# A two-block network with routed experts on one core: VectorE sums the even gathered rows, GpSimd scales and adds the odd ones

## What is computed

```python
def one_block(xb):                                   # 128 tokens
    q = (xb @ w_query).reshape(tb, PEER_HEADS, 2, PEER_KEY_DIM // 2)
    s = jnp.einsum('thpd,hpnd->thpn', q, sub_keys)
    ...                                              # per head the best 16 of 128 x 128 experts
    gate = jax.nn.softmax(best_s, axis=-1)
    u = jnp.take(expert_down, eid, axis=0)
    act = jax.nn.gelu(jnp.einsum('thkd,td->thk', u, xb), approximate=False)
    v = jnp.take(expert_up, eid, axis=0)
    return jnp.einsum('thk,thkd->td', gate * act, v)
```

## Time and profile before

| | us |
|---|---|
| median of 3 runs | 3384.24 (3382.91 to 3390.31) |
| profiled execution | 3385.41 |
| its span in the trace | 3383.5 |

### The profile page before, as it was taken

One profiled execution on the slowest core, in us unless ns is written; L12 is line 12 of the kernel. 1 busy time (PEld: TensorE's weight loads), 2 busy tenths in 40 slices (PEclk: granted clock), 3 DMA queues, 4 the chain that ended last, 5 costly groups with the idle time before them and its releaser, 6 DMA issues.

```text
span 3383.5 us, 48188 instructions
## 1 busy us (share of the span) xinstructions
PE 3248.1 (96%) x16264; PEld 1958.5 (58%) x16264; DVE 2223.6 (66%) x4855; ACT 1193.5 (35%) x3181; POOL 833.5 (25%) x686
## 2 busy tenths in 40 slices
PE   9999998999999999989999999999899999999997
PEld 4444567656666666656445544456755666666664
DVE  2064698997888776773133400269899778877777
ACT  1141105895445550011022200110589545555001
POOL 0000244433333333320000000024443333333332
PEclk9999999999999999989999999999999999999998
DMA  4153227999999999982211122122899999999997
GB/s 175 75 224 137 75 87 311 387 414 395 418 416 415 398 400 421 422 357 88 82 50 56 62 75 74 62 108 88 315 384 418 394 396 422 417 401 400 419 422 321
DMA packets 130830, 929.03 MB, mean 275 GB/s; under 512 B 15072, under 2 KB 15968, under 8 KB 19072
## 3 DMA queue, kind: packets, MB, share of 16 engines
q0 software_dynamic: 73728, 536.90, 38.7%
q1 hardware_dynamic: 53280, 379.61, 28.3%
q10 hardware_dynamic: 3680, 10.84, 0.9%
HBM read 925.17 MB, written 2.12 MB: 274 GB/s over the span
## 4 chain that ended last, share of the span: by engine, by line
PE 54%; DMA 14%; DVE 9%; issue 9%; ACT 1%; DVEq 1%; POOL 1%; POOLq 0%; ACTq 0%
PE proj L560 17%; PE proj L854 14%; DMA ring<-in_experts,idx 14%; PE obk L845 8%; PE proj L552 4%; PE proj L778 3%; DVE ring L1740 3%; DVE xn L1757 3%; PE tps L807 2%; PE proj L916 1%; PE tps L980 1%; PE obk L959 1%; PE proj L742 1%; PE proj L949 1%; DVE hT L1776 1%
## 5 line engine op out<-in xcount | busy, mean ns | idle before, releaser
L468 POOL DMA_INDIRECT ring<-in_experts,idx x512 | 679.3, 1327 | 1225.5 <-DVE xn L1757 1117.3
L854 PE MATMUL proj<-wring,hT 128*128 128x512 f32 x2048 | 948.8, 607 | 14.6 <-DVE hT L1799 14.0
L1740 DVE SCALAR_TENSOR_TENSOR ring<-ring,xn 128x1024 f32<-128x1024 f32 x512 | 608.5, 1221 | 174.1 <-DMA ring<-in_experts,idx 170.3
L845 PE MATMUL obk<-hT,wring 128*128 128x256 f32 x3072 | 694.2, 379 | 0.0
L845 PEld LDWEIGHTS obk<-hT,wring 128*128 128x128 f32 x3072 | 583.5, 190 | 159.7 <-issue 86.8
L1757 DVE SCALAR_TENSOR_TENSOR xn<-ring,coef,xn 128x1024 f32<-128x1024 f32 x512 | 628.7, 1280 | 20.9 <-DVE coef L1747 1.0
L854 PEld LDWEIGHTS proj<-wring,hT 128*128 128x128 f32 x2048 | 377.0, 192 | 397.9 <-issue 375.0
L1222 ACT ACTIVATE hot<-iotab,away 128x128 bf16<-128x128 bf16 x1792 | 548.6, 391 | 0.1
L560 PE MATMUL proj<-hT,wring 128*128 128x512 f32 x1120 | 487.3, 592 | 0.0
L489 POOL TENSOR_TENSOR ring<-ring 128x2048 bf16<-128x2048 bf16 x14 | 56.8, 4059 | 1264.3 <-DVE ring L1700 1264.3
L560 PEld LDWEIGHTS proj<-hT,wring 128*128 128x128 f32 x1120 | 211.4, 190 | 257.1 <-issue 256.8
(11 more groups left out here) (290 smaller groups left out, 2319.9 us busy)
## 6 DMA issues: line engine op xcount, KB each, us to landing
wring<-in_slabs SPq DMA_DIRECT2D x355, 1024.0 KB, 8.9
ring<-in_experts,idx POOLq DMA_INDIRECT x512, 10.1
x_res<-in_x SPq DMA_DIRECT2D x4, 512.0 KB, 13.5
ring<-in_keys ACTq DMA_DIRECT2D x2, 1024.0 KB, 6.8
out<-x_res SPq DMA_DIRECT2D x4, 512.0 KB, 2.6
ring<-ada_rows ACTq DMA_DIRECT2D x1, 1536.0 KB, 6.4
hT<-in_xT SPq DMA_DIRECT2D x1, 1024.0 KB, 10.5
ring<-in_norm_pre ACTq DMA_DIRECT2D x2, 512.0 KB, 10.4
```

The costliest lines, as they stand in the source:

```text
L468: pool.indirect_dma_start(rows[:, r, :], None, d[f"experts{layer + 1}"], bass.IndirectOffsetOnAxis(idx[:, k, r:r + 1], 0)).then_inc(row[r] ...
L845: m = pe.matmul(obk[:, j % 2, 0:DT], wring[:, k, at + c * P:at + (c + 1) * P], hT[:, c, GB * P:T], start=(c == 0), stop=(c == DC - 1))
L854: m = pe.matmul(proj[:, 2 * b + c, :], coefs[:, b * P:(b + 1) * P], wring[:, k, at + c * 512:at + (c + 1) * 512], start=False, stop=False, ...
L1740: v.scalar_tensor_tensor(rows[:, r, 0:D], rows[:, r, 0:D], 1.0, xn[:, r % GB, :], ALU.mult, ALU.mult, accum_out=dots[:, r:r + 1]).then_inc ...
```

## The change

GpSimd gets the sums of the odd rows. For each odd row it runs a TENSOR_SCALAR, the `v` half times the coefficient, in place, and a TENSOR_TENSOR that adds the result to `gathered[:, 1, :]`, with waits between them on new counters. VectorE's `row_sums` does only even rows, into `gathered[:, 0, :]`. `slot_free` becomes `even_summed` and `odd_summed`; a gather waits for the counter of its own parity. GpSimd's odd sums for a group of the unit before stand directly ahead of that group's three gathers of the next unit. The rest of the diff moves the initial counts.

```diff
+                def odd_sums(u, r, h):
+                    pool.wait_ge(coef_done, u * 2 + (layer * GROUPS + h + 1))
+                    pool.sem_inc(sum_paced, 1)
+                    pool.tensor_scalar(rows[:, r, D:2 * D], rows[:, r, D:2 * D], coef[:, r:r + 1], None, ALU.mult).then_inc(odd_scaled, 1)
+                    pool.wait_ge(odd_scaled, u * GROUP + (layer * HALF_ROWS + r // 2 + 1))
+                    pool.sem_inc(sum_paced, 1)
+                    pool.wait_ge(odd_summed, u * GROUP + (layer * HALF_ROWS + r // 2 + GROUP))
+                    pool.sem_inc(sum_paced, 1)
+                    pool.tensor_tensor(gathered[:, 1, :], gathered[:, 1, :], rows[:, r, D:2 * D], ALU.add).then_inc(odd_summed, 1)
...
                     for r in range(n):
-                        pool.wait_ge(slot_free, u * RING + (layer * GB * SLOTS + r + 1))
+                        if before is not None and r % GROUP == 0:
+                            for o in range(r, r + GROUP):
+                                if o % 2:
+                                    odd_sums(before, o, r // GROUP)
+                        pool.wait_ge(odd_summed if r % 2 else even_summed, u * GROUP + (layer * HALF_ROWS + r // 2 + 1))
                         pool.sem_inc(paced, 1)
                         pool.indirect_dma_start(
...
-                with pool.Fori(0, UNITS // 2) as it:
+                unit(0, 0, RING, None)
+                with pool.Fori(0, UNITS // 2 - 1) as it:
                     for k in range(2):
-                        unit(it * 2 + k, k, RING)
-                unit(UNITS, 0, TAIL)
+                        unit(it * 2 + (k + 1), (k + 1) % 2, RING, it * 2 + k)
+                unit(UNITS - 1, 1, RING, UNITS - 2)
+                unit(UNITS, 0, TAIL, UNITS - 1)
+                for r in range(1, TAIL, 2):
+                    odd_sums(UNITS, r, 0)
...
                 for r in range(h * GROUP + first, h * GROUP + n):
-                    v.wait_ge(slot_free, u * RING + (layer * GB * SLOTS + r - 1 + RING))
-                    v.scalar_tensor_tensor(gathered[:, r % GB, :], rows[:, r, D:2 * D], coef[:, r:r + 1], gathered[:, r % GB, :],
-                                           ALU.mult, ALU.add).then_inc(slot_free, 1)
+                    if r % 2 == 0:
+                        v.wait_ge(even_summed, u * GROUP + (layer * HALF_ROWS + r // 2 + GROUP))
+                        v.scalar_tensor_tensor(gathered[:, 0, :], rows[:, r, D:2 * D], coef[:, r:r + 1], gathered[:, 0, :],
+                                               ALU.mult, ALU.add).then_inc(even_summed, 1)
```

More of the change, by code:

```diff
@@ L38 @@
 UNITS, TAIL = divmod(GB * SLOTS, RING)
+HALF_ROWS = SLOTS
 GROUPS = 2 * UNITS + 1
@@ L343, in build @@
         z_done, z_act, coef_t_ready = sem("z_done"), sem("z_act"), sem("coef_t_ready")
-        slot_free, acc_done, acc_free = sem("slot_free"), sem("acc_done"), sem("acc_free")
+        acc_done, acc_free = sem("acc_done"), sem("acc_free")
+        even_summed, odd_summed, odd_scaled, sum_paced = sem("even_summed"), sem("odd_summed"), sem("odd_scaled"), sem("sum_paced")
         zeros_set, out_ready, paced = sem("zeros_set"), sem("out_ready"), sem("paced")
@@ L458, in gather, with unit @@
                 pool.sem_inc(paced, 1)
-                def unit(u, k, n):
+                def odd_sums(u, r, h):
[7 more added lines that the diff above has]
+                    pool.tensor_tensor(gathered[:, 1, :], gathered[:, 1, :], rows[:, r, D:2 * D], ALU.add).then_inc(odd_summed, 1)
+                def unit(u, k, n, before):
                     pool.tensor_copy(idx[:, k, 0:n], flat[:, bass.ds(u * RING, n)]).then_inc(idx_ready, 1)
@@ L1454, in _ @@
                 root(rstd[:, tb:tb + 1], ss[:, tb:tb + 1], D, rms_done)
-            act.wait_ge(slot_free, 2 * GB * SLOTS + RING)
+            act.wait_ge(even_summed, 2 * HALF_ROWS + GROUP)
+            act.wait_ge(odd_summed, 2 * HALF_ROWS + GROUP)
             for tb in range(GB):
@@ L1476, in _ @@
             v.memset(epsc2, EPS * EPS)
-            for k, (s, n) in enumerate(((mm_free, 4), (key_done, 4), (key_free, 4), (slot_free, RING), (spread_done, 2),
+            for k, (s, n) in enumerate(((mm_free, 4), (key_done, 4), (key_free, 4), (even_summed, GROUP), (odd_summed, GROUP), (spread_done, 2),
                                         (spread_free, 2), (z_act, 4), (coef_t_ready, 2))):
-                v.memset(zeros[:, 80 * k:80 * (k + 1)], 0.0).then_inc(s, n)
+                v.memset(zeros[:, 72 * k:min(72 * (k + 1), P + 512)], 0.0).then_inc(s, n)
             v.memset(silz[:, :, :], 0.0)
@@ L1861, in experts @@
                 row_sums(layer, UNITS, 0, TAIL)
-                v.wait_ge(slot_free, (layer + 1) * GB * SLOTS + RING)
+                v.wait_ge(even_summed, (layer + 1) * HALF_ROWS + GROUP)
+                v.wait_ge(odd_summed, (layer + 1) * HALF_ROWS + GROUP)
             def summed(tb):
```

## The result

The changed kernel takes 4117.63 us (median of 4 runs, 4105.14 to 4123.09), the kernel before 3386.72 (3382.91 to 3390.31): a ratio of 1.215, 95% interval 1.2135 to 1.2168. The prediction had 3743 us and a range to 3990. The direction and the mechanism held, the size did not: 731 us were lost, not 358.

What follows compares the result with a forecast made beforehand. TensorE or DMA set the pace; GpSimd's odd sums ahead of the gathers would cost, per layer, rounds 16, pass 0 41, pass 1 57, pass 2 30, pass 3 32, end 3: 179, twice 358, on 3385.4: 3743 us, range 3530 to 3990.

Steps and rivals of the forecast that it cites:

- What bounds the kernel before: Expert layer: TensorE or DMA set the pace, GpSimd idles 1117.3 us; VectorE's relief brings at most 14 us a layer.
- The price of the add: GpSimd's TENSOR_TENSOR per odd row, 128x1024 float32: 2.1 us if time goes by elements, 4.1 if by bytes; 2.1 taken.
- The price of the scale: GpSimd's TENSOR_SCALAR per odd row, not in the trace: 1.3 us taken, between 1.2 and 2.1.
- The sum behind it: Unit times from these prices, both layers: 29.5 us in rounds, 29.0 pass 0, 26.5 passes 1 and 2, 26.0 pass 3.
- the ring's chain: Passes 1 to 3: odd sums, gathers, landing, dot, gelu, tile, coefs of one ring place take 25.7 us; GpSimd's queue 25.8.
- Exclusion both ways: GpSimd's SBUF reads and VectorE's two-input instructions stop each other for their whole length; full 3.4 us per odd row.
- GpSimd waits, VectorE does not: Rival: only GpSimd is held up, rounds keep their time, pass 0 takes about 25 us a unit; 3577 us, chance 0.20.
- GpSimd starves: Rival: gathers lose 2.4 us behind VectorE, or adds cost 4.1; 30 us a unit, 3993 us, chance 0.19.
- Nearly fits: Rival: waits behind VectorE vanish, GpSimd needs 19.6 us a unit, only pass 1 pays; 3427 us, chance 0.06.
- faster: Rival: landing nearer 5.4 us, chain under 21.75 us a unit, only the rounds' relief left; 3357 us, chance 0.05.
- The range: Whole kernel: 3530 to 3990 us, from below the rival of one-sided waiting to the starving case.
- TensorE's granted clock: Expert layer: 0.97 to 1.00 before; the sum falls if it drops in TensorE's longer gaps.

Runs made afterwards that it cites:

- e4: Changed kernel with both GpSimd instructions of an odd row replaced by MEMSETs of the same size, which read nothing: 3402.1 us.
- e8: Kernel before, all sums on VectorE, plus twelve needless MEMSETs a unit on GpSimd behind the gathers: 3393.2 us.
- e9: Changed kernel with GpSimd's instructions cut to the predicted lengths, 410 columns scaled and 910 added: 3764.6 us.
- e5: Changed kernel with four chained MEMSETs per odd row, 6.1 us, in place of the scale and add: 3924.7 us.
- e11: Changed kernel, same numbers, with the scale written as a two-input TENSOR_TENSOR with the coefficient repeated along the columns: 3923.0 us.
- e7: Kernel before, all sums on VectorE, plus five needless TENSOR_TENSORs a unit that read, on GpSimd behind the gathers: 3638.1 us.

## Why the prediction was wrong in size and right in kind

- **What bounds the kernel before**: borne out. e4 and e8, which add 6 to 7 us of GpSimd's time a unit without reading, cost 14 and 7 us: GpSimd had that room, and VectorE's relief (three sums less a unit in e4) brought nothing.
- **The price of the add**: 2.1 us, measured 2.34 at least; the elements count, not the bytes. The Trainium skill's figure (GPSIMD Engine Reference, section 3.1), halved to an estimate of 2.25, was nearer than the bf16 rows of this kernel.
- **The price of the scale is the step that failed.** "I take 1.3, since one input is half the reading", between 1.2 and 2.1 us. It is 2.84 us, outside the bounds. The upper bound rested on the thought that one input can't cost more than two; no row bore it out, and it is false on this engine (2.51 ns a column against 2.11). The Trainium skill (GPSIMD Engine Reference, section 4.1) says that one-input operations are roughly line-rate on GpSimd; the 2842 ns speak against it for this instruction.
- **The sum behind it** held for passes 1 and 2, where the ring's chain and GpSimd's queue set the pace. e9 gave the kernel the forecast's prices and took 3764.6 us for 3743, with 26.5 us a unit in pass 1. That the total came so near is in part luck: the rounds and pass 0 were put 1.2 and 0.9 us a unit too high, and the forecast took 22.2 us a unit for pass 0 before, where the same cut in both traces gives 23.5; pass 2 was put too low. With the true prices, 1.54 + 0.24 us more a row, GpSimd's queue of 25.8 us a unit becomes 31.1; measured are 30.7 to 33.8.
- **Exclusion both ways**: right, and it was the riskier guess. But its price was taken as the full length of both instructions. The add holds VectorE nearly throughout, the scale for about a third (0.98 of 2.84 us), and e5 and e11 show that the holding matters little where GpSimd's queue sets the pace. In the first two stages this error and the scale's price offset each other in part: pass 0 has 30.7 us a unit, where full holding with 5.2 us a row would give 29.0 + 5.4 = 34.4. Its 30.7 is about GpSimd's queue, 31.1.
- **The rivals**: "GpSimd waits, VectorE does not" is out (1632 ns, e7). "GpSimd starves" had 30 us a unit and 3993 us and is the nearest, for a reason of its own that did not occur: the scale waits 0.80 us on the mean (3643 less 2842 ns) and the add 0.23 (2571 less 2338), near the forecast's 0.6 and far from 2.4. "Nearly fits" and "faster" are out.
- **The range** was too narrow because its top came from rivals with other mechanisms at the taken price, not from the price's own upper end. An odd row at 6.2 us, which stood in the text as an upper bound, would have given some 4450 by the same sum (2.8 us more for three rows in each of 84 units: 3743 + 706). The scale's own upper bound of 2.1 us would not have been enough: it gives some 3945, inside the range.
- **TensorE's granted clock** fell from 0.97 to 1.00 to 0.85 to 0.93 in the stages, as the prediction feared. It looks like an effect more than a cause: VectorE's L1822 waits for ScalarE's results of TensorE's tiles 63.1 us now, its forerunner L1799 waited 111.9 before. And of the 365 us by which the five stages grew, TensorE's busy time has only 97 (923.4 to 1020.4 us for the same work), its idle time the other 268. No run separates the clock, so its part inside the 97 us stays open.

## What to carry to other kernels

Before work goes to GpSimd, look at what stands behind it in GpSimd's queue. Here each microsecond of sums was a microsecond in front of the gathers that refill the ring, and idle time of an engine is only room as long as its next task's deadline is not in it. Bound the price of an operation that the trace doesn't show by its own measurement, or let the range carry the whole ignorance; here the one-input instruction was the dearer one. Elementwise work that reads SBUF on GpSimd also did not run beside VectorE's two-input work: an add took 2.21 us of VectorE's time when they met and a scale 0.98, and GpSimd itself waited behind VectorE. GpSimd's writes held nothing and waited for nothing, but they too cost queue (e5).

## What the runs showed of the hardware

- GpSimd's TENSOR_SCALAR in float32 costs 0.27 us and 2.51 ns a column (2842 ns for 1024), its TENSOR_TENSOR 0.18 us and 2.11 ns (2341), the latter with an operand repeated along the row 1890 ns in all, a MEMSET 951 (1805 for 2048).
- GpSimd's reads and VectorE's two-input instructions exclude each other both ways: a dot of 1.22 us took 2.75 behind an add. The add holds VectorE for 2.21 of 2.34 us, the scale for 0.98 of 2.84. MEMSETs neither wait nor hold (951 to 962 ns in 512 places, VectorE at 1223 ns).
- A gather's instruction also waits: 0.93 us at least, 1.08 on the mean in e5, where VectorE idles for 949 us, 1.29 in the changed kernel and 1.33 before.
